# Sums over partitions of VectorE's modulation products: transposes and a free-axis reduce in place of matmuls with a column of ones

## What is computed

```python
cond = silu(c)                               # c_ctx for the context tokens, c for the latents
shift, scale, gate, ... = cond @ w_ada + b_ada   # (1024) x (1024, 6 * 1024), per layer
h = rmsnorm(x, w) * (1 + scale) + shift
x = x + gate * mixer(h)
```

## Time and profile before

| | us |
|---|---|
| median of 3 executions | 2077.5 (2077.29 to 2085.51) |
| the profiled execution | 2075.03 |
| its span in the trace | 2073.5 |
| PE busy | 1957.8 |
| DVE busy | 1217.5 |
| ACT busy | 563.9 |
| POOL busy | 69.5 |

### The profile page before, as it was taken

The page is one execution under the profiler, slowest core; times in us unless marked ns, Lnnn a source line. Parts: engine busy times, 40 slices in busy tenths (PEclk is TensorE's granted clock), DMA queues, the critical chain, the costliest instruction groups (busy, mean ns, idle before and its releaser), DMA issues.

```text
span 2073.5 us, 32367 instructions
## 1 busy us (share of the span) xinstructions
PE 1957.8 (94%) x13099; PEld 1849.8 (89%) x13099; DVE 1217.5 (59%) x1924; ACT 563.9 (27%) x721; POOL 69.5 (3%) x120
## 2 busy tenths in 40 slices
PE   6899988879999999998999999999998999999997
PEld 4898775879999999997889889899898999999997
DVE  5776547786766766665655655655567225225335
ACT  2224553132211211223332332323233221221221
POOL 0001220000000000001010010010000000000000
PEclk8899999989999999998999999999998999999998
DMA  8522014325433533423122122121212222222211
GB/s 283 153 64 85 19 42 122 92 69 150 142 102 109 154 122 102 132 72 111 61 73 81 61 89 64 61 90 64 70 51 61 61 81 80 63 81 81 65 58 51
DMA packets 213536, 185.29 MB, mean 89 GB/s; under 512 B 10865, under 2 KB 198705, under 8 KB 213425
## 3 DMA queue, kind: packets, MB, share of 16 engines
q1 hardware_dynamic: 209504, 172.27, 27.0%
q0 software_dynamic: 3616, 11.29, 1.6%
q10 hardware_dynamic: 305, 0.10, 0.0%
HBM read 176.42 MB, written 7.21 MB: 89 GB/s over the span
## 4 chain that ended last, share of the span: by engine, by line
PE 87%; DVE 8%; ACT 2%; issue 2%; DMA 1%; SPq 1%; ACTq 0%; DVEq 0%
PE acc L595 63%; PE acc L1014 4%; PE acc L1045 2%; PE acc L1061 2%; PE acc L621 2%; PE acc L795 2%; PE mix L1034 1%; PE mix L638 1%; PE mix L765 1%; PE mix L1014 1%; PE acc L784 1%; DVE h_lo L1575 1%; PE mix L659 1%; PE mix L674 1%; PE acc L608 1%
## 5 line engine op out<-in xcount | busy, mean ns | idle before, releaser
L595 PE MATMUL acc<-h_hi,w_hi 128*128 128x320 f32 x2144 | 497.1, 313 | 21.1 <-DVE qk L2101 6.1
L595 PE MATMUL acc<-h_lo,w_hi 128*128 128x320 f32 x2144 | 492.0, 311 | 0.0
L595 PE MATMUL acc<-h_hi,w_lo 128*128 128x320 f32 x2144 | 491.8, 311 | 0.0
L1118 ACT ACTIVATE w_hi<-raw 128x2048 fp32r<-128x2048 f32 x112 | 214.2, 1914 | 654.8 <-PE acc L595 651.0
L595 PEld LDWEIGHTS acc<-h_hi,w_hi 128*128 128x128 f32 x2144 | 359.2, 189 | 28.1 <-issue 21.2
L595 PEld LDWEIGHTS acc<-h_lo,w_hi 128*128 128x128 f32 x2144 | 361.4, 189 | 0.0
L595 PEld LDWEIGHTS acc<-h_hi,w_lo 128*128 128x128 f32 x2144 | 361.0, 189 | 0.0
L1503 DVE TENSOR_TENSOR w_lo<-raw,w_hi 128x2048 fp32r<-128x2048 f32 x112 | 256.7, 2292 | 172.9 <-ACT w_hi L1118 168.9
L1954 DVE TENSOR_TENSOR gu<-silu_g,acc 128x640 f32<-128x640 f32 x44 | 36.2, 822 | 251.3 <-PE acc L595 246.0
L1597 DVE SCALAR_TENSOR_TENSOR xT<-acc,mod,xT 128x128 f32<-128x128 f32 (+2 forms) x288 | 108.9, 434 | 124.2 <-PE acc L595 122.0
L1622 DVE SCALAR_TENSOR_TENSOR tbuf<-ada_raw,scond,tbuf 128x256 f32<-128x256 f32 x392 | 172.7, 482 | 7.0
(11 more groups left out here) (325 smaller groups left out, 2484.5 us busy)
## 6 DMA issues: line engine op xcount, KB each, us to landing
ada_raw<-in_l_w_ada_dram SPq DMA_DIRECT2D x68, 512.0 KB, 4.7
raw<-in_l_w_in_dram SPq DMA_DIRECT2D x64, 512.0 KB, 4.5
raw<-in_l_w_gate_dram SPq DMA_DIRECT2D x44, 512.0 KB, 4.0
raw<-in_l_w_up_dram SPq DMA_DIRECT2D x44, 512.0 KB, 5.3
raw<-in_l_w_down_dram SPq DMA_DIRECT2D x32, 512.0 KB, 4.5
raw<-in_l_w_out_dram SPq DMA_DIRECT2D x24, 512.0 KB, 4.7
raw<-in_l_w_ada_dram SPq DMA_DIRECT2D x18, 512.0 KB, 4.6
raw<-in_l_w_down_dram SPq DMA_DIRECT2D x16, 384.0 KB, 3.7
```

The source lines that it names most:

```text
L595: last = mm(acc[:, 2 * r + b, 0:HALF], w[:, k * cols + col:k * cols + col + P], x[:, k, b * HALF:(b + 1) * HALF], start=(k == 0 and n == 0 ...
L1118: act(w_hi[s][:, :], raw[s][:, :], ACT.Copy).then_inc(S[f"w_hi{s}"], ac.up(f"w_hi{s}"))
```

## The change

`ada_add` now transposes the four squares into bank 0 or 1 of `mix`, by turns, with the identity. A new step on DVE, `ada_over_partitions`, waits for `ada_turned` and reduces each 128x128 square over the free axis into four columns of `mod[l]`, one instruction from 128x512 to 128x4. It runs on the panel of the same turn in the FFN, after the low part of the product, and at j = 1 of the down panels; in layer 0 at j = 1 and j = 2, two panels each, at j = 1 each ahead of an `ada_products`. `mods` adds the bias in place for these columns, so `mods(0, 16, 48)` becomes two calls. The waits for `ada_turned` in `ada_products`, at j = 3 and in `layer1_modulation` go. What is computed stays the same.

```diff
-            def ada_add(l, n, b_):
+            def ada_add(b_):
 
                 eng.wait_ge(S["row_in"], pe.next("row_in"))
                 for b in range(2):
                     for c in range(2):
-                        last = mm(ADA[:, l, bass.ds(n * 2 + b, 1), c:c + 1].rearrange("p o c -> p (o c)"),
-                                  ada_sum[b_][:, c, b * P:(b + 1) * P], ones[:, 0:1], start=True, stop=True)
+                        last = eng.transpose(mix[:, b_, (2 * b + c) * P:(2 * b + c + 1) * P], ada_sum[b_][:, c, b * P:(b + 1) * P], ident[:, :])
                 last.then_inc(S["ada_turned"], pe.up("ada_turned"))
...
-            def mods(l, a, b):
-
-                tt(mod[l][:, a:b, :], ADA[:, l, a:b, :],
+            def mods(l, a, b, summed=False):
+
+                tt(mod[l][:, a:b, :], mod[l][:, a:b, :] if summed else ADA[:, l, a:b, :],
                          b_ada[:, l, a:b].unsqueeze(2).broadcast_to([P, b - a, 2]), ALU.add).then_inc(S["mod_read"], v.up("mod_read"))
...
                 eng.wait_ge(S[f"ada_in{s}"], v.next(f"ada_in{s}", 32))
-                eng.wait_ge(S["ada_turned"], v.now("ada_turned", 1))
                 for k in range(KT):
...
                 eng.sem_inc(S["row_in"], v.told("row_in"))
-                v.skip("ada_turned")
+
+            def ada_over_partitions(l, n, b_):
+
+                eng.wait_ge(S["ada_turned"], v.next("ada_turned"))
+                out = mod[l][:, bass.ds(2 * n, 2), :].rearrange("p b c -> p (b c)")
+                eng.tensor_reduce(out, mix[:, b_, :].rearrange("p (o n) -> p o n", o=4), X, ALU.add).then_inc(S["dve"], v.up("dve"))
+                eng.wait_ge(S[v.last], v.ended())
...
-                for _ in range((1, 2, 0, 0, 0, 0, 0, 0)[j]):
+                if j == 0:
                     ada_products()
+                if 1 <= j < 3:
+                    for n in (ADA_DVE[0] + 2 * j - 2, ADA_DVE[0] + 2 * j - 1):
+                        ada_over_partitions(0, n, n % 2)
+                        if j == 1:
+                            ada_products()
...
-                if j == 3:
-                    eng.wait_ge(S["ada_turned"], v.now("ada_turned"))
...
-            eng.wait_ge(S["ada_turned"], v.next("ada_turned", 12))
-            mods(0, 16, 48)
+            eng.wait_ge(S["ada_turned"], v.next("ada_turned", len(ADA_PE)))
+            mods(0, 16, 24, True)
+            mods(0, 24, 48)
...
                             ins.then_inc(S["gu_ready"], v.up("gu_ready"))
                             eng.wait_ge(S[v.last], v.ended())
+                            if l == 0:
+                                ada_over_partitions(1, i * 2 + s + f0 + m, (s + m) % 2)
                     for j in range(4):
...
                             into_x(l, 1, 2 * j + c)
+                        if l == 0 and m < 2 and j == 1:
+                            ada_over_partitions(1, f0 + nf + m, m % 2)
...
             def layer1_modulation():
-                eng.wait_ge(S["ada_turned"], v.now("ada_turned"))
-                mods(1, 0, 48)
+                mods(1, 0, 48, True)
```

More of the change, by code:

```diff
@@ L718, in _ @@
                             n = ADA_DVE[0] + ADA_PLACES.index((j, t))
-                            ada_add(0, n, n % 2)
+                            ada_add(n % 2)
                     else:
@@ L968, in gate_up @@
                     if l == 0:
-                        ada_add(1, f + s_ + m, (s_ + m) % 2)
+                        ada_add((s_ + m) % 2)
                 for m, (f0, nf) in enumerate(CHUNKS):
@@ L988, in ffn @@
                         if l == 0 and m < 2 and j == 1:
-                            ada_add(1, f0 + nf + m, m % 2)
+                            ada_add(m % 2)
             ffn(0)
@@ L1945, in ffn @@
                     if l == 0:
-                        per |= {"dve": 2 + 2 * KT, "ada_in0": 32, "ada_in1": 32, "ada_turned": 2, "row_in": 2, "ada_used": 2}
+                        per |= {"dve": 2 + 2 * KT + 2, "ada_in0": 32, "ada_in1": 32, "ada_turned": 2, "row_in": 2, "ada_used": 2}
                     with v.loop(nf // 2, per) as i:
```

## The result

| | before | after |
|---|---|---|
| median of the first runs, us | 2077.4 (4) | 2059.9 (4) |
| ratio, 95% interval | | 0.9906 [0.9878, 0.9934] |
| the profiled execution, us | 2075.03 | 2059.71 |
| its span, us | 2073.5 | 2058.1 |

The changed kernel is 17.5 us faster, 0.94%. Forecast were 2068.8 us, a range of 2064 to 2075, and a chance of 0.63 for a time within 0.5% of the one before. The direction is right, the gain forecast (8.7 us) is half of the measured one, and the time lies under the range.

A forecast was written before the change was run, and what follows sets the result against it. PE was taken to bound the FFN. Saving 8.25 us there (8.05 + 0.5 - 0.3) and 0.45 in layer 0, together 8.7, takes 2075.03 to 2066.3; carrying over the 2.5 us to the median gives 2068.8, range 2064 to 2075.

The forecast's parts named there:

- DVE's remaining wait: In a layer 0 FFN gate/up turn, DVE's 2.74 us wait for PE was to shrink to 1.4 to 1.6 us.
- two of the three places where DVE becomes late: Forecast as late: FFN's first down panels of chunks 0 and 1 (0.3 us in all), and layer 0's chain (+0.75 us).
- 0.45 were forecast: Layer 0's four panels: -0.35 + 0.75 - 0.5 - 0.35, a net gain of 0.45 us.
- a margin of 1 us: Layer 0: panel 11's sums were to end near 110 us, before PE asks for them at about 111.
- The saving per panel is 0.79 - 0.44 = 0.35 us.: PE at full clock: four column products take 0.79 us in the chain, four transposes 0.44, saving 0.35 per panel.
- a rival: "More than forecast", chance 0.28: larger PE gains, including more than 0.79 us exposed per column-product group; 10.5 to 12 us off, 2066.
- I take 0.5 us for the two slow panels.: PE at half clock, one panel in layer 0 and the FFN's first: 0.5 us saved each, bounds 0.35 and 1.0.
- its ends: The bounds of the sum, 2066.0 and 2070.5 us, with 2 us added at either end for run-to-run slow-clock shifts.
- I take 0.3 us in all: PE stalls at the first down panels of FFN chunks 0 and 1: nothing to 0.35 us, twice, taken as 0.3 together.
- 8.05: PE's saving in layer 0's FFN: 23 panels at 0.35 us each.

The follow-up runs named there:

- the same with its code shifted: Kernel before with 120 semaphore increments ahead of PE's first instruction, so the head loop stands where it does in the changed kernel, modulo 256; 2078.65 us, ratio 1.0013.
- its third profile: Changed kernel unaltered, run again for comparison beside the version with both DVE orders changed; 2060.13 us, ratio 0.9914 to the kernel before.
- the kernels with eight pieces per group of Experiments 2: Changed kernel with each panel's four transposes made twice (0.87 us per group, span 2076.1), or replaced by plain identity matmuls, each issued twice (0.89 us per group).
- the kernel before with hidden increments: Kernel before with 40 semaphore increments behind each of three norms where PE waits for DVE anyway; 2074.26 us against 2077.52, ratio 0.9979.

## Why the prediction was wrong

**Right.** That PE is the bound in the FFN and that its time there is the kernel's; the transpose at 0.11 us and issued once; the reduce at 0.69 us; DVE's remaining wait (1.4 to 1.6 forecast, 1.36 measured); two of the three places where DVE becomes late. In layer 0 the chain of the changed kernel has just the reduces that were to come into it (start, us, what):

```profile
94.16 0.04 DVE w_lo L1502
...
96.37 0.69 DVE mod L1630
...
97.09 0.63 DVE tbuf L1618 x2
...
104.36 0.70 DVE mod L1630
...
112.33 0.66 PE mix L638 x4
```

Relative to the start of the projections, their end came at 142.2 to 142.5 us in four profiles of the changed kernel and at 142.7 to 143.2 in three of the kernel before: 0.6 us gained where 0.45 were forecast. But the second reduce is in the chain too, and panel 11's sums aren't ready when PE asks (0.31 us of wait before its transposes), where a margin of 1 us had been forecast. The number is close by luck.

**Wrong, by term of the sum:**

- *"The saving per panel is 0.79 - 0.44 = 0.35 us."* It is 0.45. The term was read between two marks of the chain that leave out the last of eight steps (the prediction's 0.098 us each are 0.11), and the pair of tiles behind was not compared with pairs that have no products beside them, although both numbers, 14.19 and 14.11, stood in the earlier trace rows; I put them into a rival and not into the sum. 22 panels at 0.11 are 2.4 us.
- *"I take 0.5 us for the two slow panels."* In the FFN's, 2.0 us were measured between the first two profiles, but most of it is the clock. Windows over the panel with its pair, columns as in the earlier trace rows, in the kernel before, the same with its code shifted, the changed kernel, and its third profile:

```profile
463.25:481.54 18.29, 18.29 (x107) 18.29 (x107) 10.63 (x19) 1.44 (x2) 0.00 (x0) 0.82 0.66 203
473.63:490.43 16.80, 16.80 (x107) 16.80 (x107) 10.63 (x19) 1.44 (x2) 0.00 (x0) 0.90 0.61 193
463.32:479.62 16.30, 16.30 (x102) 16.29 (x103) 11.32 (x20) 1.44 (x2) 0.00 (x0) 0.90 0.59 178
467.40:482.14 14.74, 14.74 (x102) 14.73 (x103) 11.33 (x20) 1.45 (x2) 0.00 (x0) 1.00 0.57 157
```

  At the same mean granted clock of 0.90 the saving is 0.5 us, as forecast (the kernels with eight pieces per group of Experiments 2 take 16.70 and 16.81 at 0.90). The other 1.5 us are a longer stretch at the lower clock in the kernel before, which two of its three profiles have (18.29 and 17.96 us, at 0.82 and 0.83). Whether the change shortens that stretch or it fell so is open. The sum had nothing for it; only its ends had 2 us for such shifts.
- *"I take 0.3 us in all"* for the down panels. They take 0.9: the wait itself is 0.25 and 0.13 us, inside the bounds given, but the pair behind each takes 0.24 us more, for which the sum had nothing. The last chunk takes 0.3 more, a wait that I had not looked for.
- *Missing altogether:* the place of the code in PE's program, 4.2 us, the largest single miss. The prediction counted an instruction that isn't issued only by the time it had taken. Of the idle times at the loop's turn the trace of before had all three, as "issue", and I didn't ask what they hang on.

The FFN's terms, 8.05 and 2.4 and 2.0 less 1.2, make 11.25 us, and 11.3 were measured. With the heads' 4.2 and layer 0's 0.6 they are 16.1 of the 17.5; the rest is within the scatter of layer 0's stage. With the code's place equal (the kernel before with hidden increments, 2074.26 us less the 1.8 that they cost, against 2060.13) the change itself is worth some 12 us, for 8.7 forecast. The Trainium skill (TensorE: Matmul & The Clock Gate, Part 4: PE-mode transpose) gives about 275 ns for a transpose in a kernel; that is its duration, 272 ns in the median here, and what the chain pays is 109 ns. That transposes don't keep the clock up, as the section has it, no run here shows: the clock stayed at full level in all turns with them. Of the heads' turns, the Trainium skill (Runtime: NRT & Kernel Launch, Instruction fetch mechanics) has the mechanism, a fetch at a taken branch whose target is outside the window held; the traces agree, with 88 transfers against 60. It puts this window at two pages; measured here is more, since a loop of 1754 instructions, nearly seven of its blocks of 256, ran three turns without a transfer.

## What to carry to other kernels

To sum over partitions on a full PE, count what each form issues: here an fp32 product was issued twice and a transpose once, and each piece cost 0.11 us whether it had one column or 128. Compare the tiles beside the operation, not only the operation: a part of its price stood with the pair behind. Where a kernel has long loops on PE, any edit ahead of them that changes the number of instructions can give or take microseconds far away, so look at idle time put down to "issue" at the loop's turn and at the transfers of the instruction queue before crediting the edit. And when PE's share of a turn shrinks, DVE's deadlines at the seams between loops come nearer by as much as PE gained and DVE took on; moving one block behind the first reader took the wait away here. Where PE meets a stage with its clock still rising, compare only profiles with the same mean clock there.

## What the runs showed that I had not expected

- A loop of 1754 PE instructions runs its turn without idle time at one place of the code (last instruction at 180 modulo 256) and with 1.2 to 1.9 us at four others (36, 60, 110, 240). At the first, no code is transferred for three turns.
- A semaphore increment on PE takes 153 ns from start to start: 120 of them take 18 us, of which the first transpose, which had waited until 10.9 us anyway, shows 8.6. Forty behind a norm lengthened waits of 3.2 to 3.8 us by 0.5 to 0.8, twenty by nothing.
- The same program's stage of attention and scan differs by 4 us between profiles (393.3 to 397.5), and the pair behind PE's first wait in the FFN by 1.6 us.
